# Expert weights of a two-block model: 1 MB transfers with 4 and 8 KB rows replaced by 2 MB transfers with 16 KB rows

## The reference

```
aff = softmax(h @ w_router)                    # h: 512 x 1024, 16 experts
g, idx = top_k(aff.T, 64)                      # each expert picks 64 tokens
xe = h[idx]                                    # 16 x 64 x 1024
hid = silu(xe @ w_gate[e]) * (xe @ w_up[e])    # w_gate, w_up: 16 x 1024 x 2048
ye = (hid @ w_down[e]) * g                     # w_down: 16 x 2048 x 1024
x = x.at[idx].add(ye)
out = rms_norm(x) * norm_f_g
```

## Time and profile before

| | |
|---|---|
| median of 3 runs | 2244.92 us (2244.07 to 2252.76) |
| the profiled execution | 2245.47 us |
| its span in the trace | 2243.6 us |
| mean granted TensorE clock | 0.958 of full speed |
| TensorE matmul busy | 2007.4 us (89%) |
| VectorE, ScalarE, GpSimd busy | 737.6, 544.8, 84.7 us |
| moved by DMA | 500.07 MB in 100458 packets |
| ring transfers | 384 of 1024 KB, about 20 us from issue to landing |

### The profile page before, as it was taken

How to read it: one execution, slowest core, us unless ns; L and a number is a source line. 1 busy time by engine, 2 the same in 40 slices (tenths; PEclk the granted TensorE clock), 3 DMA queues, 4 the chain that set the end, 5 groups by cost and what they waited for, 6 DMA issues and landing times.

```text
span 2243.6 us, 23438 instructions
## 1 busy us (share of the span) xinstructions
PE 2007.4 (89%) x9482; PEld 1291.9 (58%) x9482; DVE 737.6 (33%) x1096; ACT 544.8 (24%) x820; POOL 84.7 (4%) x67
## 2 busy tenths in 40 slices
PE   8999999999986998567998699999999999999996
PEld 6777788888864776435887544444444443344442
DVE  6434544333449434864432411111011111111112
ACT  4434422222433232165441200000000000000001
POOL 2000000000135000000000100000000000000000
PEclk9999999999997999777999699999999999999998
DMA  4221232322312220001336099999999999999997
GB/s 167 84 71 60 106 94 98 100 94 95 102 66 75 81 83 1 0 29 33 108 103 261 36 417 417 418 417 417 417 417 418 418 418 418 418 419 418 417 418 286
DMA packets 100458, 500.07 MB, mean 223 GB/s; under 512 B 10272, under 2 KB 10656, under 8 KB 67504
## 3 DMA queue, kind: packets, MB, share of 16 engines
q1 hardware_dynamic: 100080, 499.09, 56.6%
q10 hardware_dynamic: 320, 0.17, 0.0%
HBM read 497.13 MB, written 2.10 MB: 223 GB/s over the span
## 4 chain that ended last, share of the span: by engine, by line
PE 70%; DMA 12%; DVE 10%; issue 4%; ACT 3%; SPq 1%; POOL 0%; DVEq 0%; ACTq 0%; POOLq 0%
PE ps L1817 21%; PE ps L1929 13%; DMA ring<-in_w_up_e 11%; PE ps L2139 10%; PE ps L2158 9%; PE ps L2121 5%; PE ps L1941 2%; DVE x L1738 1%; PE ps L1790 1%; DMA ring<-in_w_down_e 1%; PE ps L2174 1%; SPq L723 1%; PE ps L1868 1%; PE ps L1865 1%; PE ps L2077 1%
## 5 line engine op out<-in xcount | busy, mean ns | idle before, releaser
L2139 PE MATMUL ps<-ring,xe 128*64 128x512 f32 x2048 | 455.7, 598 | 48.7 <-DMA ring<-in_w_up_e 24.6
L2139 PEld LDWEIGHTS ps<-ring,xe 128*64 128x64 f32 x2048 | 146.5, 137 | 356.4 <-issue 283.7
L2158 PE MATMUL ps<-ring,hidT 128*64 128x512 f32 x1024 | 225.3, 597 | 15.0 <-DVE hidT L1734 13.1
L1817 PE MATMUL ps<-n_hi,d_hi 128*128 128x512 f32 x448 | 175.5, 392 | 1.5 <-DVE d_lo L1156 0.8
L1817 PE MATMUL ps<-n_hi,d_lo 128*128 128x512 f32 x448 | 174.4, 389 | 0.0
L1817 PE MATMUL ps<-n_lo,d_hi 128*128 128x512 f32 x448 | 174.3, 389 | 0.0
L1457 DVE TENSOR_TENSOR hid<-sg,ps 128x512 f32<-128x512 f32 x32 | 20.6, 683 | 456.8 <-PE ps L2139 456.8
L1156 DVE TENSOR_TENSOR d_lo<-d_raw,d_hi 128x1024 fp32r<-128x1024 f32 x107 | 135.2, 1274 | 107.5 <-ACT d_hi L812 107.5
L2158 PEld LDWEIGHTS ps<-ring,hidT 128*64 128x64 f32 x1024 | 86.1, 138 | 144.0 <-issue 123.3
L1738 DVE TENSOR_TENSOR x<-x,ps 128x1024 f32<-128x1024 f32 x64 | 73.8, 1216 | 267.9 <-PE ps L2174 267.9
L1929 PE MATMUL ps<-h_hi,w_hi 128*128 128x512 f32 x296 | 119.6, 404 | 25.4 <-DVE h_lo L1160 17.9
(11 more groups left out here) (401 smaller groups left out, 2609.2 us busy)
## 6 DMA issues: line engine op xcount, KB each, us to landing
ring<-in_w_gate_e SPq DMA_DIRECT2D x128, 1024.0 KB, 19.2
ring<-in_w_up_e SPq DMA_DIRECT2D x128, 1024.0 KB, 20.8
ring<-in_w_down_e SPq DMA_DIRECT2D x128, 1024.0 KB, 20.9
d_raw<-in_tiles_in SPq DMA_DIRECT2D x107, 512.0 KB, 3.4
raw<-in_tiles_in SPq DMA_DIRECT2D x53, 512.0 KB, 3.5
raw<-in_tiles_in SPq DMA_DIRECT2D x16, 256.0 KB, 3.0
x_in<-in_xT_in SPq DMA_DIRECT2D x4, 512.0 KB, 6.8
x<-in_xT_in SPq DMA_DIRECT2D x1, 2048.0 KB, 7.4
```

The costliest lines, as they stand in the source:

```text
L1817: mm = pe.matmul(bank, lt[:, n, k0 + k, :], rt[:, k, :], start=k == 0 and m == 0, stop=k == gr.nk - 1 and m == 2)
L2139: mm = pe.matmul(ps[half * CAP:(half + 1) * CAP, 2 * m + q, :], xe[:, k, :], ring[:, n % RING, (2 * q + half) * S:(2 * q + half + 1) * S], ...
L2158: mm = pe.matmul(ps[d * CAP:(d + 1) * CAP, 4, :], hidT[:, q, c, half * CAP:(half + 1) * CAP], ring[:, n % RING, j * D + d * S:j * D + (d + ...
```

## The change

The ring keeps its 96 KB per partition but is cut into six slots of 16 KB per partition; a transfer moves 2 MB, and an expert needs 12 of them. So that a partition's 16 KB are contiguous in memory, the rows are dealt out in another way:
- gate and up: partition p holds rows 8p to 8p + 7 of the 1024, and transfer n takes two of these eight. The rows of neighbouring partitions lie 64 KB apart in memory.
- down: a transfer holds 512 rows, partition p rows 4p to 4p + 3 of them, the whole 2 MB contiguous in memory.

The contraction must then meet its rows in the same order: the gather takes every eighth column of `h2` as stationary operand (`h2[:, t, k::KD]`, a step of 32 bytes), and the transposes take every fourth column of `hid` (`c::4`, a step of 16 bytes). The number and shapes of the matmuls are as before. TensorE waits for a chunk, and gives a slot back, once for every eight float32 matmuls where it was four. SyncE issues half as many transfers for the experts.

The helper `Steps.wait(eng, name, i)` is written as `eng.wait_ge(steps.sem, steps.count(name, i))` throughout, with the same values; of those lines one pair stands below.

```diff
-RING = 12
+RING = 6
...
-    def wait(self, eng, name, i=0):
-        eng.wait_ge(self.sem, i * len(self.names) + (self.index[name] + 1))
+    def count(self, name, i=0):
+
+        return i * len(self.names) + (self.index[name] + 1)
...
-                    lo_dve.wait(sp, "lo1", TT - 1)
+                    sp.wait_ge(lo_dve.sem, lo_dve.count("lo1", TT - 1))
...
-        ring = at("ring", [P, RING, FF], 64)
+        ring = at("ring", [P, RING, 2 * FF], 64)
...
-        gate_v = w_gate_e_2[0].rearrange("e (k p) f -> p e k f", p=P)
-        up_v = w_up_e_2[0].rearrange("e (k p) f -> p e k f", p=P)
-        down_v = w_down_e_2[0].rearrange("e (c j p) d -> p e c j d", p=P, j=2)
-        PER = 24
+        gate_v = w_gate_e_2[0].rearrange("e (p k) f -> p e k f", p=P)
+        up_v = w_up_e_2[0].rearrange("e (p k) f -> p e k f", p=P)
+        down_v = w_down_e_2[0].rearrange("e (b p c) d -> p e b c d", p=P, c=4)
+        PER = 12
...
-                    src = gate_v[:, e, n, :] if n < 8 else up_v[:, e, n - 8, :] if n < 16 else down_v[:, e, n - 16, :, :]
-                    dst = ring[:, s, :] if n < 16 else ring[:, s, :].rearrange("p (j d) -> p j d", j=2)
+                    if n < 4:
+                        src = gate_v[:, e, 2 * n:2 * n + 2, :]
+                    elif n < 8:
+                        src = up_v[:, e, 2 * n - 8:2 * n - 6, :]
+                    else:
+                        src = down_v[:, e, n - 8, :, :]
+                    dst = ring[:, s, :].rearrange("p (j d) -> p j d", j=2 if n < 8 else 4)
...
-                used(act, e, 7)
+                used(act, e, 3)
...
-                used(act, e, 23)
+                used(act, e, 11)
...
-                used(dve, e, 15)
+                used(dve, e, 7)
...
-                        mm = pe.matmul(ps[:, 7, k * CAP:(k + 1) * CAP], h2[:, t, k * P:(k + 1) * P], pick[:, t, :],
+                        mm = pe.matmul(ps[:, 7, k * CAP:(k + 1) * CAP], h2[:, t, k::KD], pick[:, t, :],
...
-                        chunk(e, n)
+                        if k % 2 == 0:
+                            chunk(e, n // 2)
...
+                                at_ = k % 2 * FF + (2 * q + half) * S
...
-                                               ring[:, n % RING, (2 * q + half) * S:(2 * q + half + 1) * S],
+                                               ring[:, n // 2 % RING, at_:at_ + S],
...
-                        mm.then_inc(s_free[n % RING], 1)
+                        if k % 2:
+                            mm.then_inc(s_free[n // 2 % RING], 1)
...
-                        mm = pe.transpose(ps[:, 5 + q, c * P:(c + 1) * P], hid[:, q, c * P:(c + 1) * P], ident[:, :])
+                        mm = pe.transpose(ps[:, 5 + q, c * P:(c + 1) * P], hid[:, q, c::4], ident[:, :])
...
-                    chunk(e, n)
+                    if i % 2 == 0:
+                        chunk(e, n // 2)
...
-                    mm.then_inc(s_free[n % RING], 1)
+                    if i % 2:
+                        mm.then_inc(s_free[n // 2 % RING], 1)
```

More of the change, by code:

```diff
@@ L753, in _ @@
             for k in range(1, KD):
-                o1_act.wait(pool, f"sq{k}")
+                pool.wait_ge(o1_act.sem, o1_act.count(f"sq{k}"))
                 if k > 1:
-                    o1_pool.wait(pool, f"sum{k - 1}")
+                    pool.wait_ge(o1_pool.sem, o1_pool.count(f"sum{k - 1}"))
                 a = psq[:, 0, :] if k == 1 else pacc[:, :]
@@ L935, in _ @@
                 split1(n)
-            u_pe.wait(act, "sum")
-            set_pool.wait(act, "eps")
+            act.wait_ge(u_pe.sem, u_pe.count("sum"))
+            act.wait_ge(set_pool.sem, set_pool.count("eps"))
             u_act.done(act.activation(R[:, :], ps[:, 7, :], ACT.Sqrt, bias=eps[:, :], scale=1.0 / D), "root")
@@ L996, in mqk @@
                 if n >= 2:
-                    mq_dve.wait(act, "c4", n - 2)
+                    act.wait_ge(mq_dve.sem, mq_dve.count("c4", n - 2))
                 read(st, j, i, scr[n % 2 * 4][:, 2:S + 2], ACT.Copy)
@@ L1089, in _ @@
                     n, h = k - 2, DW[k - 2][0]
-                    d_pe.wait(act, f"o{n}")
+                    act.wait_ge(d_pe.sem, d_pe.count(f"o{n}"))
                     for c in range(TT):
@@ L1343, in _ @@
                 split1(n)
-            u_pe.wait(dve, "sum")
-            u_act.wait(dve, "root")
+            dve.wait_ge(u_pe.sem, u_pe.count("sum"))
+            dve.wait_ge(u_act.sem, u_act.count("root"))
             u_dve.done(dve.reciprocal(R[:, :], R[:, :]), "R")
-            u_dve.wait(dve, "R")
+            dve.wait_ge(u_dve.sem, u_dve.count("R"))
             for gr in STREAM:
@@ L1428, in residual @@
                 return evac
-            n2_dve.wait(dve, "lo7")
+            dve.wait_ge(n2_dve.sem, n2_dve.count("lo7"))
             for n in range(2):
@@ L1450, in _ @@
             run("mqk", mqk)
-            x3_pool.wait(dve, f"x{KD - 1}")
+            dve.wait_ge(x3_pool.sem, x3_pool.count(f"x{KD - 1}"))
             mq_pad.done(dve.memset(m_tok[:, :, :, MD:MD + 1], 1.0), "col")
@@ L1461, in link @@
                 steps.done(ins, name)
-                steps.wait(dve, name)
+                dve.wait_ge(steps.sem, steps.count(name))
             def way(t, d):
@@ L1648, in _ @@
                     n = k - 1
[L1649 removed]
+                    dve.wait_ge(d_act.sem, d_act.count(f"e1_{n}"))
                     link(d_dve, dve.reciprocal(small(n, 6, 2), small(n, 4, 2)), f"rec{n}")
@@ L1743, in _ @@
             expert(NE - 1, more=False)
-            z_act.wait(dve, "root")
+            dve.wait_ge(z_act.sem, z_act.count("root"))
             link(z_dve, dve.reciprocal(esm[:, 32:36], esm[:, 20:24]), "rstd")
@@ L1784, in group1 @@
                         if i == 0:
-                            h_dve.wait(pe, f"lo{k}")
+                            pe.wait_ge(h_dve.sem, h_dve.count(f"lo{k}"))
                         n = gr.tiles[k // 2] % SLOTS
@@ L1887, in chain @@
                 if (name, i) == ("q", 2):
-                    u_pool.wait(pe, f"sum{KD - 1}")
+                    pe.wait_ge(u_pool.sem, u_pool.count(f"sum{KD - 1}"))
                     u_pe.done(pe.matmul(ps[:, 7, :], ones[:, :], xacc[:, :], start=True, stop=True), "sum")
@@ L1911, in _ @@
                 chain(gr.name, gr.i)
-            pl_pool.wait(pe, f"b{KD - 1}")
+            pe.wait_ge(pl_pool.sem, pl_pool.count(f"b{KD - 1}"))
             read_done(pe, "proj", 6)
@@ L1979, in _ @@
                 kt_pe.done(mm, f"kt{c}")
-            r_act.wait(pe, "e3")
+            pe.wait_ge(r_act.sem, r_act.count("e3"))
             for c in range(TT):
@@ L1993, in keys @@
                     if n >= 4:
-                        l_dve.wait(pe, f"w{n - 3}")
+                        pe.wait_ge(l_dve.sem, l_dve.count(f"w{n - 3}"))
                     for c in range(TT):
@@ L2021, in _ @@
                     if n:
-                        l_dve.wait(pe, f"tmp{n - 1}")
+                        pe.wait_ge(l_dve.sem, l_dve.count(f"tmp{n - 1}"))
                     for c in range(TT):
@@ L2030, in scores @@
                 if n >= 2:
-                    d_dve.wait(pe, f"m1_{n - 2}")
+                    pe.wait_ge(d_dve.sem, d_dve.count(f"m1_{n - 2}"))
                 for i in range(2):
@@ L2057, in _ @@
                 f_pe.done(mm, f"t{h}")
-            f_dve.wait(pe, "t3")
+            pe.wait_ge(f_dve.sem, f_dve.count("t3"))
             for k in range(TURNS):
@@ L2097, in _ @@
                 t_pe.done(mm, f"x{t}")
-            t_dve.wait(pe, "x0")
-            t_act.wait(pe, "x0")
+            pe.wait_ge(t_dve.sem, t_dve.count("x0"))
+            pe.wait_ge(t_act.sem, t_act.count("x0"))
             for t in range(TT):
@@ L2104, in _ @@
             t_pe.done(mm, "logits")
-            t_dve.wait(pe, "aff")
+            pe.wait_ge(t_dve.sem, t_dve.count("aff"))
             for t in range(TT):
@@ L2108, in _ @@
             t_pe.done(mm, "affT")
-            t_dve.wait(pe, "sel")
+            pe.wait_ge(t_dve.sem, t_dve.count("sel"))
             for t in range(TT):
@@ L2129, in expert @@
             def expert(e, more=True):
-                x_act.wait(pe, "xe", e)
+                pe.wait_ge(x_act.sem, x_act.count("xe", e))
                 for m in range(2):
@@ L2167, in expert @@
                 e_pe.done(mm, "place")
-                e_act.wait(pe, "place", e)
+                pe.wait_ge(e_act.sem, e_act.count("place", e))
                 for t, b in enumerate((5, 0, 2, 5)):
                     if t == 3:
-                        e_dve.wait(pe, "o0", e)
+                        pe.wait_ge(e_dve.sem, e_dve.count("o0", e))
                     for d in range(2):
@@ L2175, in expert @@
                     e_pe.done(mm, f"o{t}")
-                e_dve.wait(pe, "o2", e)
+                pe.wait_ge(e_dve.sem, e_dve.count("o2", e))
             gather(0)
```

469 lines of the change are left out of this document (234 added, 235 removed).

## The result

| | before | changed |
|---|---|---|
| median of 4 runs, in turn on one chip | 2244.89 us | 2374.15 us |
| ratio, 95% interval | | 1.0567 (1.0543 to 1.0591) |
| profiled span | 2243.6 us | 2372.9 us |
| mean granted clock | 0.958 | 0.906 |

The account below looks back on a forecast made before the run. The prediction took the stream of expert weights to bound the kernel; -22.8 us for rate, +2.3 for the later start and +1.8 for the larger last piece gave -18.7, so 2226.8 us, range 2218 to 2280 us.

Parts of the forecast that it names:

- Bound now: Expert loop: the stream of weights, 418 GB/s over 820 us, sets the end; TensorE has 19 us of slack.
- Rate: Expert weight stream: 16 KB rows raise 409 and 422 GB/s to 428, a gain of 22.8 us.
- The two ends: Ends of the weight stream: it starts 2.3 us later, and the larger last piece of down adds 1.8 us.
- Coarser slots in the loop at nothing: Ring inside the expert loop: the transfer queue stays fed with 2 MB slots, so no cost.
- The gather and the transposes read with a step, taken as nothing: TensorE's stepped loads in gather and transposes: room for a load half as productive, so 0 us taken.
- The upper bound: Stepped loads in gather and transposes: at most 6.6 us and 0.9 us more, from loads at half pace.
- The rival: Gather and transposes: stepped loads at half pace, 7.5 us in each of 15 turns, 2335 us; chance 0.16.

Follow-up runs that it names:

- experiments 1 and 2: Changed kernel with gather and transposes read in plain order (wrong features), 2228.95 us, ratio 0.9915; with only the gather plain, 2228.62 us.
- the first kernel of 7: Changed kernel with the writers of `h2` and `hid` regrouping them and TensorE reading both plain, full reference computed: 2228.48 us, ratio 0.9911.
- the first run: Changed kernel with both the gather and the transposes read in plain order, wrong features: 2228.95 us, ratio 0.9915.

## Why the prediction was wrong

- *Bound now*: right. The stream set the end, and only 19 us of slack stood between it and TensorE.
- *Rate*: right. 428 GB/s were taken, 428 measured in the loops of experiments 1 and 2 and of the first kernel of 7; rows of 4, 8 and 16 KB at 409, 422 and 428, no cost for the pitch, none of the gain from the transfer's size.
- *The two ends*: right in kind, +2.7 and +1.7 us for +2.3 and +1.8. The coarse ring alone gave 0.1% more, 2 to 3 us by two medians.
- *Coarser slots in the loop at nothing*: right. The loop's mean of 428 GB/s in the first run leaves no room for a queue run dry.
- *The gather and the transposes read with a step, taken as nothing*: this step failed. The load was set against the matmuls of the projection, one float per 0.44 ns, and called half as fast, so with room to spare. But those floats come four to a 16-byte line, one line in 1.77 ns. A stepped load wants a line for each float, one in 0.89 ns, and nothing in the trace showed that pace. Counted in lines, the same row would have spoken for a load twice as long; measured were 1.88 ns for each float (241 ns for 128). The range had left out what this step could cost at its upper bound.
- *The upper bound* of that step, 6.6 + 0.9 us per expert, was also short: measured were 11.0. The loads cost 8.1; the transposes' step next to nothing, 0.12; and 2.8 came from the clock, which was in no term. I had named what the slow load delays, not what TensorE's clock does while it loads and hardly multiplies.
- *The rival* of loads at half pace was the right mechanism, with a chance of 0.16 and 2335 us. Its price was 7.5 x 15 + 14.8 = 127 us on a TensorE-bound span of 2205.6; measured are 15 x 11.03 for the loop (a period of 68.26 us in the later experts, less 57.23), and for the first gather 1.6 in place of 13.9, since the plain loads were slow already at half clock (13.90 us against 15.49). That is 165 us in the loop and a loop that began 2.9 us later, 1.6 of them the first gather: 2205.6 + 165.5 + 2.9 = 2374.0 by that sum, for a span of 2372.9.

## What to carry to other kernels

When a new layout of weights makes TensorE read its stationary operand with a step, price the load first: at a step of 8 bytes it took 5% more here, at 12 bytes half as much again, from 16 bytes on about twice the time, and a gather bound by its loads has nothing to hide that under. Then ask what the slower load does to TensorE's clock. Let the writer of the operand do the regrouping instead; it writes once where TensorE reads once per expert, and here nearly all of its cost vanished behind other work. Count a read's pace in lines, not in floats, before saying that there is room. Longer rows do pay on a stream that sets the end: 4, 8 and 16 KB gave 409, 422 and 428 GB/s, and doubling the transfer with the old rows gave nothing.

## What the runs showed of the hardware

- A stepped float32 weight load has a pace of its own: 241 ns for 128 columns at 32 bytes, at a granted clock of 0.50 and at mixed clocks alike, where the plain load follows the clock (217 and 114 ns). At 12 bytes it was 173 ns at full clock and 213 at half.
- The same step of 16 bytes added 15 ns to a transpose (0.12 us for eight) and 122 ns to a float32 matmul's load.
- TensorE's granted clock fell from full to half while its records showed it busy without a gap: slow loads (173 to 241 ns at full clock) with 64 columns of multiplication between them. With 256 columns in between, at the step of 32 bytes, it stayed full, and so it did with 64 columns between loads of 120 ns.
- ScalarE's copy of 128x1024 floats with its input read at a step of 32 bytes took 2.07 us where the plain one takes 1.06 (8.27 and 4.25 us for four); VectorE's product of 128x512 floats took 1046 ns for 683 when it wrote neighbouring numbers 512 bytes apart, its inputs read plain.
